# 300 in place of 165 gather slots ahead of the first dense search, 18 in place of 22 among the searches

## The chip, the cores and the metric

The kernel runs on one core of one Trainium2 chip. The metric is the device time of one execution in microseconds (us). The core has TensorE (PE, matmuls and transposes), VectorE (DVE), ScalarE (ACT), GpSimd (POOL), SyncE (SP, which issues most of the DMAs) and 16 DMA engines that all queues share.

## The reference

One decoder layer in float32 for 1,024 tokens of width 1,024: differential attention of 8 heads beside a multi-scale pooling branch, sigmoid gates, an output projection and a first layer norm (the mixer); then PEER, a mixture of 16,384 experts of one neuron each; then a second layer norm. PEER, cut to what matters here:

```python
q = (yb @ w_q).reshape(PEER_CHUNK, PEER_HEADS, 2, PEER_HALF)
s = jnp.einsum('chpk,hpnk->chpn', q, sub_keys).astype(jnp.float32)
s1, i1 = lax.top_k(s[:, :, 0], PEER_TOPK)
s2, i2 = lax.top_k(s[:, :, 1], PEER_TOPK)
cand = (s1[..., :, None] + s2[..., None, :]).reshape(PEER_CHUNK, PEER_HEADS, PEER_TOPK * PEER_TOPK)
sc, ci = lax.top_k(cand, PEER_TOPK)
...
idx = row * PEER_KEYS + col
gate = jax.nn.softmax(sc, axis=-1)
act = jax.nn.gelu(jnp.einsum('ched,cd->che', u[idx], yb), approximate=False)
return jnp.einsum('che,ched->cd', (gate * act).astype(yb.dtype), v[idx])
```

Each token picks 8 x 16 = 128 experts; `u` and `v` have 16,384 rows of 1,024 numbers.

## The kernel before, in words

**Two ways through PEER.** The 1,024 tokens are 8 tiles of 128. The first five tiles (`GT`) take the *gather path*: for one tile, slot 0 to 127 each fetch, for every token of the tile, one expert's `u` and `v` row from HBM into one of the 8 buffers of `ring` (128 rows of 8 KB, about 1 MB), in all 5 x 128 = 640 slots. The last three tiles (`DT`) take the *dense path*: all 16,384 experts are run through TensorE in 128 blocks, and gates that are zero nearly everywhere pick out what counts.

**What a slot costs.** POOL issues the gather (L860) once the slot eight before it has been summed. DVE multiplies and sums the `u` half with the tokens (`product`, L1565); ACT turns the dots of two slots into coefficients (Gelu at L1088, scaling at L1092); DVE adds the scaled `v` half of the slot three before to `z_e` (`add_row`, L1519). Between them DVE runs the steps of the search for the next head's top 16 (`found`, `retrieve`, L1330 to L1401), one search for 16 slots, 24 slots ahead of its first gather.

**The mixer and the dense path.** The mixer runs in three groups of 2, 3 and 3 tiles. For each group PE makes the projections (`units`, L1634, weights `w_in` in three buffers), attention (scores L1680, transposes L1699, values L1719), the branch products (L1751, L1756), the output projection (L1774), and the PEER queries and scores (L1808, L1820, weights `wq` in two buffers that SP refills at L621). In attention DVE takes the logits from PSUM (L1219), waits for ACT's exponentials (L937) at L1228 and mixes the two maps at L1237; in the branches it gates and adds (L1258, L1262, L1266). For the dense path DVE then runs 24 dense searches (`dense_found`) and writes one-hot rows and columns (`dense_hots`, L1446, L1448), from which PE makes the gate matrices (L1850); they go to `g_scr` in HBM. In the last phase PE makes, for each of 128 blocks, `dense_scores` (L1861, 16 instructions, weights `ub`, three buffers, loaded at L710) seven blocks ahead, ACT a Gelu (L1058), DVE the product with the gates (`dense_gates`, L1458), and PE `dense_sums` (L1875, 12 instructions, `vb`, four buffers, L719). The gates come back eight blocks at a time in `gq` (L737, 1.5 MB).

**What sets the order.** The program is one static list for each engine. Everything but the gather path has a due time in *ticks* (`step_at`, `branch_at`, `norm_at`, `score_at`, `sum_at` and others), and each engine's list of it is in order of ticks. The gather path is laid out by slots. `KNOTS`, four pairs (slot, tick), says by straight lines between them which tick a slot stands at (`tick_at`); after each slot every engine's list lets in the other work that is due by then (`advance(tick_at(...))`). So `KNOTS` sets how densely slots lie among the rest, and nothing else. Tick 0 is in the scores of the first group; ticks 7 to 145 hold attention of the second group, 145 to 216 its branches and norm, 216 to 312 its queries; 318 to 505 attention of the third group, 505 to 598 its branches and norm, 598 to 686 its queries; the dense searches run from 616 to 880, the one-hots from 711 to 960 or so, and block b of the dense sums stands at 960 + 9b. The last knot puts slot 640 at tick 2092, 20 before the end of the sums. Each engine works strictly in its list's order.

Of the kernel before, what the change touches and what calls it, by code (L numbers as in the profile page):

```python
# [27 lines left out]
NK = 128  # L28
# [26 lines left out]
LAST_SLOT = SLOTS * GT  # L55
# [46 lines left out]
OH_LEN = 3.5  # L102
T_D = TURN_AT[-1] + 6 + int(OH_LEN * P / NOH) + 14
BLOCK = 9
KNOTS = ((0, 0), (165, 616), (187, 880), (LAST_SLOT, T_D + BLOCK * NK - 20))


def tick_at(t):
    if t <= 0:
        return t  # L110
    for (s0, k0), (s1, k1) in zip(KNOTS, KNOTS[1:]):
        if t <= s1:
            return k0 + (k1 - k0) * (t - s0) / (s1 - s0)
    return KNOTS[-1][1] + t - LAST_SLOT

# [1816 lines left out]
```

How the kernel before makes its waits and increments, by code:

```python
    @block.sync  # L532
# [2 lines left out]
        def units(g):  # L535
            for i in range(UNITS):
                if i < RAWS:
                    yield (T_A[0] - 60 + (2 if i else 0), EARLY + 1, norm_at(1, GTS[1]) + 9)[g]
                    if g == NG - 1 and i == 0:
                        sp.wait_ge(mixed, 2 * KTS[g - 1])
                else:
                    yield unit_at(g, i - RAWS) + 3
                    sp.wait_ge(unit, UNITS * g + i - RAWS + 1)
                kind, j = SEQ[i]
                sp.dma_start(w_raw[g][i % RAWS][:], a["w_in"][FIRST_OF[kind] + j]).then_inc(w_in[g % 2][i % RAWS], 16)
# [1 line left out]
        def tokens(g):  # L547
            yield (T_A[0] - 59, EARLY, norm_at(1, GTS[1]) + 8)[g]
            if g == NG - 1:
                sp.wait_ge(mixed, 2 * KTS[g - 1])
            for c in range(DC):
                sp.dma_start(x_raw[g][:, c],
                             a["xT"][c * P:(c + 1) * P, OLD[g]:OLD[g] + WS[g]]).then_inc(x_all_in if g else x_in[c // 2], 16)
            if g == 0:
                yield unit_at(0, 0)
            elif g == 1:
                yield branch_at(0, DC) + 2
                sp.wait_ge(merge_done, DC)
            else:
                yield norm_at(1, GTS[1]) + 15
                sp.wait_ge(y1_out, 16 * len(PARKED))
# [1 line left out]
            if g == 0:  # L563
                yield unit_at(0, 2)
                sp.wait_ge(bias_made, 2)
                sp.dma_start(b_scr, bias[0][:]).then_inc(bias_in, 16)
# [215 lines left out]
        store(GT - 1)  # L782
        advance(END)
        sp.wait_ge(stored, 16 * TT)
```

## Time and profile before

| | us |
|---|---|
| median of 3 runs | 3548.49 |
| lowest and highest | 3542.34, 3552.24 |
| the profiled execution | 3545.78 |
| its span, first to last instruction | 3544.0 |

Over the span PE is busy 83%, DVE 74%, ACT 26%, POOL 25%, and the DMA engines move 292 GB/s on average. These shares are averages over stages with different limits, so the table of stages has to be read as well as the page. A stage's borders are given in us; the border for a tick is where DVE starts the product of the slot that stands at that tick. Durations of single instructions overlap by some tens of ns where they follow each other at once, so sums over a stretch are taken from the table of stages, which counts overlapping time once.

### The profile page before, as it was taken

To read this page: it belongs to the slowest core of one execution; us is meant where nothing else is said; L and a number is where in the kernel's file an instruction comes from. 1 tells how busy PE (TensorE), PEld (TensorE's weight loads), DVE (VectorE), ACT (ScalarE), POOL (GpSimd) and SP (SyncE) were. 2 spreads that over 40 slices of the span, in tenths; PEclk is the share of its full clock that TensorE was granted. 3 is DMA by queue.
4 is the path that set the end of the run, shared out by engine and by line. 5 is a ranking of instruction groups with operands and counts; after the bars stand their busy time and mean duration, and the time that the engine had idled before them with its cause. 6 is when DMAs were issued, how large, how long until landed. Compare 5 with 4: busy or idle time off the path is not lost.

```text
span 3544.0 us, 32139 instructions
## 1 busy us (share of the span) xinstructions
PE 2943.5 (83%) x9793; PEld 1744.0 (49%) x9793; DVE 2632.1 (74%) x6244; ACT 907.2 (26%) x2305; POOL 882.0 (25%) x866
## 2 busy tenths in 40 slices
PE   9999999979988889785434498878898998889896
PEld 7776665535554554454333354434444444444442
DVE  2224556674666668789999789977889888788888
ACT  2302455122344431223223221211121111112111
POOL 1101223221122322200002223323333233332332
PEclk9999999989999999895655599989999999999998
DMA  6635666787655569633336899999999999999996
GB/s 201 226 122 215 233 225 215 285 325 270 237 195 193 188 246 345 235 125 109 118 127 231 306 417 415 414 381 379 411 410 415 394 402 402 385 394 417 400 415 258
DMA packets 216235, 1034.86 MB, mean 292 GB/s; under 512 B 22400, under 2 KB 60800, under 8 KB 132224
## 3 DMA queue, kind: packets, MB, share of 16 engines
q0 software_dynamic: 92160, 671.13, 48.3%
q1 hardware_dynamic: 122896, 361.54, 27.6%
q8 instruction: 79, 1.29, 0.1%
q14 instruction: 92, 0.75, 0.1%
q10 hardware_dynamic: 1008, 0.14, 0.0%
HBM read 989.21 MB, written 43.52 MB: 291 GB/s over the span
## 4 chain that ended last, share of the span: by engine, by line
PE 58%; DMA 17%; DVE 16%; ACT 3%; SPq 2%; issue 2%; POOL 0%; DVEq 0%; ACTq 0%
PE w_ps L1634 16%; DMA ub<-uT 13%; PE w_ps L1861 13%; PE r_o L1875 7%; PE w_ps L1808 4%; PE w_ps L1875 3%; DVE z_e L1519 3%; DVE hot_r L1446 3%; PE w_ps L1774 2%; DVE hot_c L1448 2%; PE w_ps L1751 2%; DVE ring L1565 2%; DMA ring<-uv,idx 2%; SPq L719 2%; PE r_o L1719 2%
## 5 line engine op out<-in xcount | busy, mean ns | idle before, releaser
L860 POOL DMA_INDIRECT ring<-uv,idx x640 | 739.5, 1155 | 2342.0 <-DVE z_e L1519 2275.3
L1519 DVE SCALAR_TENSOR_TENSOR z_e<-ring,coef,z_e 128x1024 f32<-128x1024 f32 x640 | 820.9, 1283 | 170.0 <-ACT coef L1092 169.5
L1861 PE MATMUL w_ps<-yT,ub 128*128 128x384 f32 x2048 | 715.0, 505 | 163.6 <-DMA ub<-uT 163.6
L1565 DVE CUSTOM_DVE_ANT_0 ring<-ring,ytok 128x1024 f32<-128x1024 f32 x640 | 781.7, 1221 | 66.5 <-DMA ring<-uv,idx 65.5
L1634 PE MATMUL w_ps<-x,w 128*128 128x384 f32 (+1 forms) x2112 | 664.4, 463 | 41.9 <-ACT v L908 22.8
L1861 PEld LDWEIGHTS w_ps<-yT,ub 128*128 128x128 f32 x2048 | 403.9, 198 | 481.2 <-DMA ub<-uT 175.2
L1634 PEld LDWEIGHTS w_ps<-x,w 128*128 128x128 f32 x2112 | 396.3, 194 | 253.2 <-issue 84.6
L1875 PE MATMUL r_o<-vb,gel_d 128*128 128x512 f32 x1024 | 467.0, 599 | 46.0 <-DMA vb<-v 29.6
L1875 PEld LDWEIGHTS r_o<-vb,gel_d 128*128 128x128 f32 x1024 | 196.4, 192 | 270.4 <-issue 209.3
L1850 PE MATMUL r_o<-hot_r,hot_c 128*128 128x128 f32 x768 | 168.9, 409 | 180.1 <-DVE hot_c L1448 180.1
L1058 ACT ACTIVATE gel_d<-w_ps 128x384 f32<-128x384 f32 x128 | 62.6, 489 | 915.3 <-PE w_ps L1861 915.3
L1850 PEld LDWEIGHTS r_o<-hot_r,hot_c 128*128 128x128 f32 x768 | 156.0, 310 | 194.0 <-DVE hot_c L1448 193.8
L1875 PE MATMUL w_ps<-vb,gel_d 128*128 128x512 f32 x512 | 240.6, 592 | 0.0
L1088 ACT ACTIVATE gel<-dot 128x2 f32<-128x2 f32 x320 | 64.0, 200 | 638.9 <-DVE dot L1565 638.3
L1808 PE MATMUL w_ps<-yT,wq 128*128 128x384 f32 x512 | 184.8, 506 | 20.6 <-DMA wq<-wq 10.5
L1875 PEld LDWEIGHTS w_ps<-vb,gel_d 128*128 128x128 f32 x512 | 97.3, 190 | 122.6 <-issue 122.6
L1092 ACT ACTIVATE coef<-gel,gate 128x1 f32<-128x1 f32 x640 | 153.8, 287 | 10.4
L1808 PEld LDWEIGHTS w_ps<-yT,wq 128*128 128x128 f32 x512 | 97.1, 197 | 91.2 <-issue 22.0
L1047 ACT ACTIVATE stage_g<-r_o 128x512 f32<-128x512 f32 x96 | 97.5, 1054 | 167.9 <-PE r_o L1850 167.9
L1446 DVE TENSOR_SCALAR hot_r<-count_d,turned_d 128x128 f32<-128x128 f32 x384 | 135.8, 354 | 0.1
L1219 DVE CUSTOM_DVE_ANT_0 e<-w_ps,bias 128x512 f32<-128x512 f32 (+3 forms) x160 | 90.8, 594 | 60.6 <-PE w_ps L1680 59.0
L1228 DVE RECIPROCAL st_a<-st_a 128x2 f32<-128x2 f32 x64 | 10.5, 164 | 165.0 <-ACT e L937 164.8
(238 smaller groups left out, 2965.1 us busy)
## 6 DMA issues: line engine op xcount, KB each, us to landing
w<-w_in SPq DMA_DIRECT2D x132, 512.0 KB, 3.9
ub<-uT SPq DMA_DIRECT2D x128, 512.0 KB, 11.4
vb<-v SPq DMA_DIRECT2D x128, 512.0 KB, 14.7
g_scr<-stage_g SPq DMA_DIRECT2D x12, 2048.0 KB, 7.7
gq<-g_scr SPq DMA_DIRECT2D x16, 1536.0 KB, 39.7
wq<-wq SPq DMA_DIRECT2D x46, 512.0 KB, 4.7
wc<-w_branch SPq DMA_DIRECT2D x24, 768.0 KB, 5.6
wo<-w_out SPq DMA_DIRECT2D x24, 512.0 KB, 7.8
```

Of the source, the lines that this page charges most:

```text
L860: nc.gpsimd.indirect_dma_start(out=ring[t % RING][:], out_offset=None, in_=a["uv"], in_offset=bass.IndirectOffsetOnAxis(ap=idx[:, slot:slo ...
L1047: nc.scalar.activation(stage_g[c % 2][:, :, 4 * b:4 * b + 4].rearrange("p r t -> p t r"), place_bank(v)[:].rearrange("p (t r) -> p t r", t ...
L1092: nc.scalar.activation(coef[:, slot + j:slot + j + 1], gel[:, slot + j:slot + j + 1], ACT.Copy, scale=gate[:, h, e_:e_ + 1]).then_inc(coef ...
L1219: nc.vector.tensor_tensor_reduce(both[:, wh, c * HALF:c * HALF + n], score_bank(g, wh)[:, 0:n], bias[g][:, begin:begin + n], SCALE, NEG, A ...
L1446: nc.vector.tensor_scalar(hot_r[u % 2][:, j], count_d[:], turned_d[:, 0, t:t + 1], turned_d[:, 2, t:t + 1], ALU.is_equal, ALU.mult)
L1519: nc.vector.scalar_tensor_tensor(z[n % 2][:], ring[t % RING][:, D:], coef[:, slot:slot + 1], z[n % 2][:], ALU.mult, ALU.add).then_inc(vsum ...
L1565: nc.vector.tensor_tensor_reduce(ring[r][:, 0:D], ring[r][:, 0:D], y_of(n)[:], 1.0, 0.0, ALU.mult, ALU.add, dot[:, slot:slot + 1]).then_in ...
L1634: ins = nc.tensor.matmul(bank, w_raw[g][i % RAWS][:, c, :], x_raw[g][:, c, :], start=c == 0, stop=c == DC - 1)
L1808: ins = nc.tensor.matmul(query_bank(g)[:, 0:WS[g]], query_weights(g, i)[:, c * P:(c + 1) * P], yT[g][c // 4][:, c % 4, :], start=c == 0, s ...
L1850: ins = nc.tensor.matmul(place_bank(v)[:, j * NK:(j + 1) * NK], hot_c[u % 2][:, 4 * part + j], hot_r[u % 2][:, 4 * part + j], start=True, ...
L1861: ins = nc.tensor.matmul(dense_bank(b)[:, 0:DENSE], ub[b % NUB][:, c], yT[2][c // 4][:, c % 4, :], start=c == 0, stop=c == DC - 1)
L1875: ins = nc.tensor.matmul(sum_bank(i, half)[:], gel_d[b % NGEL][:, i * P:(i + 1) * P], vb[b % NVB][:, half * HALF:(half + 1) * HALF], start ...
```

## The change

One line, a table of numbers. Its four pairs are (slot, tick):

```diff
 BLOCK = 9
-KNOTS = ((0, 0), (165, 616), (187, 880), (LAST_SLOT, T_D + BLOCK * NK - 20))
+KNOTS = ((0, 0), (300, 616), (318, 880), (LAST_SLOT, T_D + BLOCK * NK - 20))
```

A slot now stands every 2.05 ticks instead of every 3.73 in ticks 0 to 616, every 14.67 instead of 12 in ticks 616 to 880, and every 3.76 instead of 2.68 after tick 880. PE's list is the same row for row. On DVE, ACT, POOL and SP the same work stands in another order; ACT has 164 table loads in place of 154. No instruction of the gather path itself is added or taken away.

**DVE in the second group's attention**, from one step's maximum (L1223) to the reciprocal (L1228) that waits for ACT's exponentials. A slot is one L1565 with its second row and one L1519. Before:

```order
L1223 TENSOR_REDUCE st_a<-st_a 128x2
L1565 ISA ring_222,dot<-ring_222,ytok_168 128x1024
L1565 ISA dot 128x1
L1519 SCALAR_TENSOR_TENSOR z_e_286<-ring_219,coef,z_e_286 128x1024
L1387 TENSOR_REDUCE rc<-hot 128x16
L1228 RECIPROCAL st_a<-st_a 128x2
```

After, two steps later in the same attention (`osb` is an output of attention, L1379 to L1387 are search steps):

```order
L1565 ISA ring_225,dot<-ring_225,ytok_168 128x1024
L1565 ISA dot 128x1
L1519 SCALAR_TENSOR_TENSOR z_e_286<-ring_222,coef,z_e_286 128x1024
L1379 TENSOR_TENSOR hot<-abf,i_296 128x256
L1505 TENSOR_SCALAR gate<-gate,esum 128x16
L1249 TENSOR_SCALAR osb_105<-r_o,st_a 128x128
L1565 ISA ring_226,dot<-ring_226,ytok_168 128x1024
L1565 ISA dot 128x1
L1519 SCALAR_TENSOR_TENSOR z_e_286<-ring_223,coef,z_e_286 128x1024
L1383 TENSOR_TENSOR hot<-hot,topf 128x256
L1565 ISA ring_219,dot<-ring_219,ytok_168 128x1024
L1565 ISA dot 128x1
```

Over the 24 steps of this attention one or two slots stand between L1223 and L1228 before, and one to three after.

**DVE in the third group's branches**, where PE's next product waits until the gates of the last have been made (L1258, L1262). Before, from one sum (L1266) to the next:

```order
L1266 TENSOR_TENSOR gates2a<-gates2a,gates2b 128x384
L1258 SCALAR_TENSOR_TENSOR gates2a<-gates2a,w_ps 128x384
L1565 ISA ring_222,dot<-ring_222,ytok_169 128x1024
L1565 ISA dot 128x1
L1519 SCALAR_TENSOR_TENSOR z_e_287<-ring_219,coef,z_e_287 128x1024
L1360 MAX_INDEX besti<-best,cand 128x8
L1361 MATCH_REPLACE cand_233<-best,cand 128x256
L1364 MAX best<-cand_233 128x8
L1262 SCALAR_TENSOR_TENSOR gates2b<-gates2b,w_ps 128x384
L1266 TENSOR_TENSOR gates2a<-gates2a,gates2b 128x384
```

After, the first part of the same piece:

```order
L1266 TENSOR_TENSOR gates2a<-gates2a,gates2b 128x384
L1565 ISA ring_222,dot<-ring_222,ytok_169 128x1024
L1565 ISA dot 128x1
L1519 SCALAR_TENSOR_TENSOR z_e_287<-ring_219,coef,z_e_287 128x1024
L1360 MAX_INDEX besti<-best,cand 128x8
L1361 MATCH_REPLACE cand_233<-best,cand 128x256
L1364 MAX best<-cand_233 128x8
L1258 SCALAR_TENSOR_TENSOR gates2a<-gates2a,w_ps 128x384
L1565 ISA ring_223,dot<-ring_223,ytok_169 128x1024
L1565 ISA dot 128x1
L1519 SCALAR_TENSOR_TENSOR z_e_287<-ring_220,coef,z_e_287 128x1024
```

Where one slot stood between a sum and the next, three stand now: these two, and a third after L1262.

**DVE in the dense sums**, from one block's product with its gates (L1458) back to the slots before it. Before:

```order
L1565 ISA ring_221,dot<-ring_221,ytok_169 128x1024
L1565 ISA dot 128x1
L1519 SCALAR_TENSOR_TENSOR z_e_287<-ring_226,coef,z_e_287 128x1024
L1383 TENSOR_TENSOR hot<-hot,topf 128x256
L1565 ISA ring_222,dot<-ring_222,ytok_169 128x1024
L1565 ISA dot 128x1
L1519 SCALAR_TENSOR_TENSOR z_e_287<-ring_219,coef,z_e_287 128x1024
L1387 TENSOR_REDUCE rc<-hot 128x16
L1458 TENSOR_TENSOR gel_d_272<-gel_d_272,gq_276 128x384
L1565 ISA ring_223,dot<-ring_223,ytok_169 128x1024
L1565 ISA dot 128x1
```

After, the whole piece from the block before:

```order
L1458 TENSOR_TENSOR gel_d_271<-gel_d_271,gq_276 128x384
L1565 ISA ring_221,dot<-ring_221,ytok_169 128x1024
L1565 ISA dot 128x1
L1519 SCALAR_TENSOR_TENSOR z_e_287<-ring_226,coef,z_e_287 128x1024
L1383 TENSOR_TENSOR hot<-hot,topf 128x256
L1565 ISA ring_222,dot<-ring_222,ytok_169 128x1024
L1565 ISA dot 128x1
L1519 SCALAR_TENSOR_TENSOR z_e_287<-ring_219,coef,z_e_287 128x1024
L1387 TENSOR_REDUCE rc<-hot 128x16
L1458 TENSOR_TENSOR gel_d_272<-gel_d_272,gq_276 128x384
```

Two slots stand between two blocks at this place, where there were three.

## Rows read from the trace of the kernel before

**Rows 1.** The page: span, busy time, 40 slices (clock, DMA share).

```profile
span 3544.0 us, 32139 instructions
...
PE 2943.5 (83%) x9793; PEld 1744.0 (49%) x9793; DVE 2632.1 (74%) x6244; ACT 907.2 (26%) x2305; POOL 882.0 (25%) x866
...
PEclk9999999989999999895655599989999999999998
DMA  6635666787655569633336899999999999999996
```

**Rows 2.** Busy time by stage; columns: stretch, length, busy time (instructions), clock, DMA.

```profile
core 0: us, PE busy (x) PEld busy (x) DVE busy (x) ACT busy (x) POOL busy (x), PEclk, DMA share, GB/s
308.00:492.00 184.00, 183.85 (x774) 121.37 (x773) 100.14 (x259) 78.09 (x192) 38.36 (x49) 1.00 0.67 240
492.00:634.00 142.00, 138.50 (x559) 83.21 (x558) 89.65 (x222) 74.42 (x178) 45.22 (x59) 1.00 0.62 220
634.00:763.00 129.00, 109.79 (x316) 58.51 (x314) 83.86 (x165) 19.95 (x49) 25.90 (x25) 0.94 0.78 290
763.00:900.00 137.00, 124.20 (x418) 75.09 (x419) 82.88 (x158) 29.21 (x78) 30.53 (x26) 0.95 0.82 306
905.00:1045.00 140.00, 118.72 (x461) 68.74 (x461) 82.40 (x197) 59.86 (x126) 29.64 (x35) 0.94 0.60 213
1045.00:1170.00 125.00, 107.38 (x449) 63.30 (x449) 83.64 (x201) 63.28 (x132) 33.03 (x41) 0.95 0.57 195
1170.00:1305.00 135.00, 117.55 (x479) 69.77 (x477) 86.20 (x196) 65.51 (x140) 38.91 (x44) 0.96 0.55 193
1305.00:1369.00 64.00, 60.60 (x183) 35.33 (x184) 50.03 (x102) 5.60 (x20) 17.49 (x18) 0.97 0.98 376
1369.00:1450.00 81.00, 63.20 (x173) 31.39 (x172) 67.02 (x122) 17.23 (x46) 26.93 (x22) 0.87 0.85 321
1450.00:1866.00 416.00, 237.16 (x938) 176.84 (x936) 380.28 (x1488) 105.27 (x181) 21.26 (x22) 0.72 0.36 127
1866.00:2024.00 158.00, 60.52 (x261) 55.11 (x262) 139.92 (x415) 48.63 (x85) 42.29 (x29) 0.54 0.73 263
2024.00:3507.00 1483.00, 1311.39 (x3448) 669.29 (x3446) 1267.71 (x2384) 266.69 (x857) 490.10 (x421) 0.94 1.00 403
```

**Rows 3.** The gate product L1458 and the slots' L1519 in the dense sums, alone.

```profile
2024.00:3507.00 1483.00, 69.66 (x126) 0.94 1.00 403
...
2024.00:3507.00 1483.00, 540.54 (x422) 0.94 1.00 403
```

**Rows 4.** The chain of waits inside the dense sums: start us, us, what.

```profile
2104.40 5.16 PE w_ps L1861 x16
2109.56 3.43 PE r_o L1875 x8
2112.99 1.72 PE w_ps L1875 x4
2114.71 5.16 PE w_ps L1861 x16
...
2214.47 8.25 SPq L719
...
2222.77 34.05 DMA ub<-uT
```

**Rows 5.** DMA in the dense sums: packets, MB, share; issues, KB each, us to landing.

```profile
q0 software_dynamic: 60480, 440.43, 72.4%
q1 hardware_dynamic: 61378, 156.92, 27.5%
...
vb<-v SPq DMA_DIRECT2D x124, 512.0 KB, 16.4
ub<-uT SPq DMA_DIRECT2D x118, 512.0 KB, 12.6
gq<-g_scr SPq DMA_DIRECT2D x14, 1536.0 KB, 39.8
ring<-uv,idx POOLq DMA_INDIRECT x418, 11.8
```

**Rows 6.** DMA issues in the second group's queries (763 to 900 us), us to landing.

```profile
wq<-wq SPq DMA_DIRECT2D x14, 512.0 KB, 6.2
```

**Rows 7.** Waits in the second group's attention and branches (308 to 763 us).

```profile
POOL ring L860 <- DVE z_e L1519: 321.0, 44, 18.4
...
DVE st_a L1228 <- ACT e L937: 75.3, 20, 9.1
ACT aT L950 <- PE w_ps L1699: 40.1, 19, 4.7
DVE osb L1249 <- PE r_o L1719: 29.3, 17, 7.2
DVE e L1219 <- PE w_ps L1680: 27.2, 11, 14.0
```

**Rows 8.** Table loads of ACT at the Gelu of slots, from the page's groups.

```profile
L1088 ACT ACT_TABLE_LOAD x76 | 97.5, 1283 | 1.3
```

## The prediction

> **What bounds the kernel now.** I read the page first. The DMA line of the 40 slices is at 9 from slice 24 to 39, and the clock line dips around slices 19 to 23 [rows 1]: stages with different limits. So the table of stages comes next [rows 2]. From 308 to 900 us PE is the fullest engine (183.85 of 184, 138.50 of 142, 109.79 of 129, 124.20 of 137), and it stays so until 1369 us, where DVE has a third of its time free in attention: 82.40 of 140, 83.64 of 125, 86.20 of 135. From 1450 to 2024 us (dense searches and one-hots) DVE is the limit, 380.28 of 416 and 139.92 of 158, with the DMA engines at 0.36 and 0.73. In the dense sums, 1483 us long, the DMA share is 1.00, PE is busy 1311.39 and DVE 1267.71. That stage is bound by DMA, with PE close behind. The chain there shows how it looks from PE: blocks follow each other every 10.31 us (2104.40 to 2114.71: 5.16 of scores, 3.43 + 1.72 of sums), until a wait for `ub` of 34.05 us after SP has hung 8.25 us in issuing a `vb` load [rows 4]. The transfer in front of them is `gq`, 39.8 us to land, once in eight blocks [rows 5].
>
> **Prices of a slot.** DVE: in the dense sums 1267.71 us less 69.66 of gate products, over 422 slots [rows 2, 3], is 2.84 us a slot, its share of a search included. DMA: the gather queue took 72.4% of 1483 us for 422 slots [rows 3, 5], 2.54 us of all 16 engines a slot. The other queue took 27.5%, 408 us.
>
> **What moves.** Slots per tick change from 0.268 to 0.487 up to tick 616, so the nine stages before 1450 us, of 72, 73, 71, 96, 62, 60, 65, 51 and 60 ticks, get 15.8, 16.0, 15.6, 21.0, 13.6, 13.2, 14.2, 11.2 and 13.2 slots more, 134; one more falls in the 6 ticks between 900 and 905 us, together 300 - 165 = 135. Ticks 616 to 880 lose 4, ticks 880 to 960 lose 29.9 - 21.3 = 8.6, and the dense sums lose the rest, 422 to about 301.
>
> **The dense sums.** DMA needs 408 + 301 x 2.54 = 1173 us. DVE needs 1268 - 121 x 2.84 = 924 us. PE needs 121 blocks of scores at 5.16 and 128 of sums at 3.43 + 1.72, 624 + 659 = 1283 us at the pace of undisturbed blocks [rows 4]. So PE takes over as the limit, and only 200 of the 310 us that DMA gives up can be had. Some of the stall behind `gq` will stay. It costs (1483 - 1311)/14 = 12 us each time now, with the gather queue never empty; with DMA asked for 73 us in the 82 that PE takes for eight blocks, I take 2 us for each of 16, an estimate near the low end, since between the 19 gathers of eight blocks the engines now have gaps that `gq` can use. The ends are 0 and 5 us. That gives 1315 us, a gain of 168 (ends 200 and 120).
>
> **Searches and one-hots.** DVE is the limit, so what it loses comes off: 4 x 2.84 = 11 us and 8.6 x 2.84 = 24 us. What covers nothing here is PE, at 237 of 416 us and 61 of 158 [rows 2]. Gain 35, ends 20 and 37.
>
> **The stages before 1450 us, without attention.** Each gets the time of its fullest resource. Busy DVE time plus 2.84 for each slot more, and DMA share times length plus 2.54 for each:
> 634 to 763 (129 us): DVE 83.9 + 44.3 = 128, DMA 100.6 + 39.6 = 140, so +11.
> 763 to 900 (137 us): DVE 82.9 + 59.6 = 142, DMA 112.3 + 53.3 = 166, so +29.
> 1305 to 1369 (64 us): DVE 50.0 + 31.8 = 82, DMA 62.7 + 28.4 = 91, so +27.
> 1369 to 1450 (81 us): DVE 67.0 + 37.5 = 104, DMA 68.9 + 33.5 = 102, so +23.
> Together +90. The first and third of these hold branches, where three slots now stand between the gates for which PE's products wait: what is queued behind a slot there is PE itself.
>
> **Attention.** Here DVE would need, out of 184, 142, 140, 125 and 135 us, 100.1 + 44.9 = 145, 89.7 + 45.4 = 135, 82.4 + 38.6 = 121, 83.6 + 37.5 = 121 and 86.2 + 40.3 = 127. It fits by the sum, but only if DVE hardly waits, and it works in order: it waits for ACT's exponentials at L1228 (75.3 us in 20 waits), for values at L1249 (29.3) and scores at L1219 (27.2) [rows 7], and PE in turn waits for what stands behind slots on DVE. What share such a mutual chain can reach no row of these stages shows; today it is 0.54 to 0.67. The nearest row in which PE and DVE are both pressed is that of the dense sums, DVE 1268 of 1483, 0.855 [rows 2]. At 0.85 the stages take 171, 159, 142, 142 and 149: 0 + 17 + 2 + 17 + 14 = +50, and since in the first of them PE has no slack at all (183.85 of 184) I add 5% of it, 9. That is +59. The lower end is +10 (DVE fills its time), the upper is below. ACT gets more Gelus between its exponentials, and each change of table is a load of 1283 ns [rows 8]; ten more loads are 13 us, and ACT has at least 62 of 125 us free. The Trainium skill, page "ScalarE: Activation LUTs", section "What ACT_TABLE_LOAD costs", puts a whole switch at about 2.66 us with the drain; by it the ten are 27 us, still beside other work. The trace has a row for the load and none for the drain.
>
> **The sum.** Gains 168 + 35 = 203, losses 90 + 59 = 149: 54 us off. The profiled execution took 3545.8 us, so 3492; the median of the runs lies 2.7 us higher, so I predict 3495.
>
> **Weights that land later.** With the gather queue as full as in the dense sums, a 512 KB load lands after 12.6 to 16.4 us, where `wq` takes 6.2 [rows 5, 6]. With two buffers, two query products need one landing and one product of about 5.16 us: at 12.6 that is 8.9 us each and 142 us for 16, inside the 166 above; at 16.4 it is 173, 7 us more. So it is in the range, not in the sum. The Trainium skill, page "DMA: Bandwidth & Descriptors", section "Queues, rings and completion order", says that each DMA engine goes round the queues that have work, a packet at a time. By that rule the SP queue's loads are slowed wherever gathers are dense, which speaks against the change before 1450 us and for it in the dense sums; it would put the sum at the 173 as well.
>
> **Rivals.**
> *Almost free in front* (0.12). DVE's free third in attention takes the slots, +10 in place of +59, and `gq` leaves no stall (1283): 200 + 35 - 90 - 10 = 135 off, 3413. For it: DVE's work fits by the sum in all five stages. Against it: DVE would have to be 0.95 busy in a chain where it stands at 0.63 now.
> *Lockstep in attention, slower* (0.28). POOL's gather of slot t waits for the sum of t - 8, DVE's sum for ACT's coefficient of three slots ago, and ACT stands in order behind PE. In ticks, these leads shrink by 3.73/2.05: three slots were 11.2 ticks and are 6.2, a little over one step of attention. If DVE reaches only 0.72, the five stages take 201, 188, 168, 168 and 176, +175 in place of +59: 265 - 203 = 62 slower, 3611. The point from which it decides: at 0.77 the stages cost about 115 and gains and losses cancel. For it: today's shares, and waits at L1228 up to 9.1 us [rows 7]. Against it: those waits are long because PE sets the pace, and slots in between fill them.
> *The dense sums do not shrink* (0.06). If the stall behind `gq` comes from `gq` itself and SP's hang and not from gathers, 12 us stay 16 times: 1283 + 192 = 1475, a gain of 8 in place of 168, and the whole is 106 slower, 3655. That would be the change doing nothing where it is meant to. Against it: 39.8 us for 1.5 MB is 40 GB/s, far from the 403 of the stage [rows 2, 5].
>
> **How the numbers follow.** The forecast has 0.54. Its own range is 3430 to 3550: the dense ends (-32, +48), attention from +10 to about the point of balance. Of that, 0.10 lies within 0.3% of before (about what a measurement of this kernel can tell from no change, 11 us) and 0.44 is faster. With the first rival, faster is 0.56; same 0.10; slower 0.28 + 0.06 = 0.34. The range for 8 in 10 must reach the lockstep case: 3430 to 3630. It leaves out most of the first rival and all of the last.
>
> **What would show it.** In the changed profile: dense sums of 1290 to 1340 us with a DMA share below 0.95, a gather count near 301, `gq` landing in under 20 us, and hardly a wait for `ub`; the one-hot stage DVE-bound and 24 us shorter; the start of the dense searches at about 1450 + 149 = 1600 us, with DVE near 0.85 busy in attention and PE below 0.9; `wq` landing in 10 us or more. The prediction is wrong if DVE in attention stays below 0.77, if `ub` waits stay at 12 us each, or if PE's granted clock falls well below the 0.94 to 1.00 of these stages, since its work would then no longer fit between DVE's.

## The result, and the profile after

| | before | changed |
|---|---|---|
| median, us | 3549.26 | 3436.98 |
| lowest to highest | 3542.34 to 3552.24 | 3435.76 to 3438.46 |
| span of the profiled execution | 3544.0 | 3435.3 |

The ratio is 0.9687 with a 95% interval of 0.967 to 0.9703: 112 us faster, where 54 were forecast. The direction was right and the time lies in the range; the forecast gain was half of what came.

The page of the changed kernel, against [rows 1]:

```profile
span 3435.3 us, 32149 instructions
...
PE 2934.8 (85%) x9793; PEld 1738.0 (51%) x9793; DVE 2622.9 (76%) x6244; ACT 915.9 (27%) x2315; POOL 907.7 (26%) x866
...
PEclk9999999997998989988966655999999999999999
DMA  6635888899987777998322257999999999999995
```

The work is the same to a fraction of a per cent; where it lies has changed. DMA is now at 7 to 9 from slice 5 to 19, and the last block of high DMA share is shorter. The table of stages of the changed kernel, with borders at the same ticks as in [rows 2], shows how much each stage has grown or shrunk:

```profile
core 0: us, PE busy (x) PEld busy (x) DVE busy (x) ACT busy (x) POOL busy (x), PEclk, DMA share, GB/s
308.00:496.00 188.00, 185.23 (x777) 121.81 (x776) 143.93 (x344) 93.77 (x226) 56.56 (x64) 1.00 0.88 321
496.00:653.00 157.00, 144.52 (x570) 86.15 (x568) 134.94 (x310) 91.25 (x216) 71.31 (x76) 0.99 0.83 302
653.00:796.00 143.00, 111.60 (x308) 58.32 (x309) 127.91 (x251) 25.03 (x73) 41.94 (x41) 0.90 0.97 386
796.00:955.00 159.00, 131.31 (x422) 78.22 (x421) 141.57 (x266) 39.00 (x113) 55.91 (x48) 0.91 1.00 401
966.00:1123.00 157.00, 119.17 (x444) 67.20 (x443) 126.28 (x284) 66.91 (x153) 49.69 (x50) 0.88 0.79 282
1123.00:1257.00 134.00, 105.71 (x438) 62.51 (x439) 119.57 (x263) 72.23 (x159) 56.97 (x56) 0.91 0.81 288
1257.00:1398.00 141.00, 119.79 (x473) 70.42 (x471) 119.90 (x265) 66.65 (x156) 56.91 (x57) 0.92 0.77 274
1398.00:1490.00 92.00, 68.55 (x189) 38.07 (x189) 85.99 (x176) 12.50 (x42) 27.61 (x28) 0.89 0.99 405
1490.00:1595.00 105.00, 72.65 (x182) 35.89 (x183) 103.17 (x193) 25.90 (x72) 40.76 (x35) 0.81 0.96 376
1595.00:1995.00 400.00, 227.60 (x921) 170.10 (x920) 366.74 (x1460) 98.51 (x165) 17.62 (x19) 0.74 0.33 124
1995.00:2133.00 138.00, 58.32 (x260) 53.68 (x260) 118.11 (x369) 46.18 (x73) 27.16 (x20) 0.55 0.67 240
2133.00:3398.00 1265.00, 1265.00 (x3424) 651.57 (x3425) 910.70 (x1707) 201.29 (x642) 363.30 (x298) 1.00 0.95 369
```

| stage | before | after | forecast growth | measured |
|---|---|---|---|---|
| five attention stages | 726 | 777 | +59 | +51 |
| branches, norm, queries of group 2 (129, 137) | 266 | 302 | +40 | +36 |
| branches, norm and first queries of group 3 (64, 81) | 145 | 197 | +50 | +52 |
| the 6 ticks between (5) | 5 | 11 | 0 | +6 |
| dense searches and one-hots | 574 | 538 | -35 | -36 |
| dense sums | 1483 | 1265 | -168 | -218 |

The sum is -109, the difference of the spans. The last row is nearly all of the miss. There PE is now busy 1265.00 of 1265 us at a granted clock of 1.00, and DMA is down to 0.95. Its DMA rows and waits, against [rows 5]:

```profile
q0 software_dynamic: 42768, 311.45, 62.7%
q1 hardware_dynamic: 59775, 154.24, 32.6%
...
vb<-v SPq DMA_DIRECT2D x123, 512.0 KB, 8.2
ub<-uT SPq DMA_DIRECT2D x118, 512.0 KB, 7.5
gq<-g_scr SPq DMA_DIRECT2D x14, 1536.0 KB, 16.2
ring<-uv,idx POOLq DMA_INDIRECT x296, 9.3
```

```profile
DVE z_e L1519 <- ACT coef L1092: 349.6, 94, 7.0
...
PE r_o L1875 <- DMA vb<-v: 28.6, 1, 28.6
```

The gate load lands in 16.2 us instead of 39.8, `ub` in 7.5 instead of 12.6, and the wait of PE for `ub` (34.05 us on the chain in [rows 4]) has left the list; one wait for the first `vb` is left, which ends where the stage begins. DVE's 349.6 us of idle time before L1519 are the room that it now has.

For the forecast it matters how many blocks of sums (L1875, 12 instructions a block) lie inside the stage. Before, and after:

```profile
2024.00:3507.00 1483.00, 672.93 (x1512) 288.08 (x1510) 0.94 1.00 403
...
2133.00:3398.00 1265.00, 660.36 (x1488) 283.68 (x1489) 1.00 0.95 369
```

That is 126 blocks before and 124 after, of 128.

### The profile page after: what moved, and what is told of

Its sections match the earlier page's. It is cut to its first block, busy times and chain, and to the rows that moved or that the text cites. A ratio compares the mean times of both kernels' runs of the same rounds, so it can differ in the third digit from the quotient of the medians.

```text
span 3435.3 us, 32149 instructions
## 1 busy us (share of the span) xinstructions
PE 2934.8 (85%) x9793; PEld 1738.0 (51%) x9793; DVE 2622.9 (76%) x6244; ACT 915.9 (27%) x2315; POOL 907.7 (26%) x866
## 3 DMA queue, kind: packets, MB, share of 16 engines
q1 hardware_dynamic: 122896, 361.54, 28.3%
## 4 chain that ended last, share of the span: by engine, by line
PE 65%; DVE 23%; DMA 6%; ACT 3%; issue 3%; SPq 0%; POOL 0%; DVEq 0%; ACTq 0%; POOLq 0%
PE w_ps L1861 19%; PE w_ps L1634 14%; PE r_o L1875 13%; PE w_ps L1875 6%; DVE z_e L1519 5%; DVE ring L1565 4%; PE w_ps L1808 3%; DVE hot_r L1446 3%; DVE hot_c L1448 2%; PE r_o L1808 2%; DMA ring<-uv,idx 2%; PE r_o L1719 1%; DMA wq<-wq 1%; PE w_ps L1680 1%; PE w_ps L1774 1%
## 5 line engine op out<-in xcount | busy, mean ns | idle before, releaser
L860 POOL DMA_INDIRECT ring<-uv,idx x640 | 752.1, 1175 | 2234.4 <-DVE z_e L1519 2173.6
L1519 DVE SCALAR_TENSOR_TENSOR z_e<-ring,coef,z_e 128x1024 f32<-128x1024 f32 x640 | 819.0, 1280 | 359.4 <-ACT coef L1092 359.2
L1565 DVE CUSTOM_DVE_ANT_0 ring<-ring,ytok 128x1024 f32<-128x1024 f32 x640 | 779.6, 1218 | 13.7 <-DMA ring<-uv,idx 13.7
L1634 PE MATMUL w_ps<-x,w 128*128 128x384 f32 (+1 forms) x2112 | 672.4, 467 | 61.0 <-ACT v L908 34.5
L1861 PE MATMUL w_ps<-yT,ub 128*128 128x384 f32 x2048 | 683.6, 488 | 0.0
L1861 PEld LDWEIGHTS w_ps<-yT,ub 128*128 128x128 f32 x2048 | 390.3, 191 | 297.4 <-issue 60.3
L1875 PE MATMUL r_o<-vb,gel_d 128*128 128x512 f32 x1024 | 462.6, 595 | 28.6 <-DMA vb<-v 28.6
L1875 PEld LDWEIGHTS r_o<-vb,gel_d 128*128 128x128 f32 x1024 | 195.3, 191 | 248.9 <-issue 187.9
L1875 PE MATMUL w_ps<-vb,gel_d 128*128 128x512 f32 x512 | 240.6, 592 | 0.0
L1875 PEld LDWEIGHTS w_ps<-vb,gel_d 128*128 128x128 f32 x512 | 97.3, 190 | 122.4 <-issue 122.4
L1751 PE MATMUL w_ps<-o,wc 128*128 128x384 f32 x256 | 93.3, 520 | 19.3 <-DMA wc<-w_branch 9.6
```

Of the source, the lines that this page charges most:

```text
L860: nc.gpsimd.indirect_dma_start(out=ring[t % RING][:], out_offset=None, in_=a["uv"], in_offset=bass.IndirectOffsetOnAxis(ap=idx[:, slot:slo ...
L1519: nc.vector.scalar_tensor_tensor(z[n % 2][:], ring[t % RING][:, D:], coef[:, slot:slot + 1], z[n % 2][:], ALU.mult, ALU.add).then_inc(vsum ...
L1565: nc.vector.tensor_tensor_reduce(ring[r][:, 0:D], ring[r][:, 0:D], y_of(n)[:], 1.0, 0.0, ALU.mult, ALU.add, dot[:, slot:slot + 1]).then_in ...
L1634: ins = nc.tensor.matmul(bank, w_raw[g][i % RAWS][:, c, :], x_raw[g][:, c, :], start=c == 0, stop=c == DC - 1)
L1751: ins = nc.tensor.matmul(bank, branch_weights(g, n)[:, j, :], o_all[g][:, j, :], start=j == 0, stop=j == CA - 1)
L1861: ins = nc.tensor.matmul(dense_bank(b)[:, 0:DENSE], ub[b % NUB][:, c], yT[2][c // 4][:, c % 4, :], start=c == 0, stop=c == DC - 1)
```

## The experiments

The reasons to be tested: (A) each stage is as long as its fullest resource; the dense sums cost the larger of PE's floor and the DMA demand of 408 us + 2.54 us a slot. (B) the stalls behind `gq` are a cost of their own. For attention: DVE's load, or the lockstep of the engines, or ACT's table switches. Each run makes one edit to the changed kernel or to the one before; one run joins two of them.

### One part of the change at a time

```diff
-KNOTS = ((0, 0), (300, 616), (318, 880), (LAST_SLOT, T_D + BLOCK * NK - 20))
+KNOTS = ((0, 0), (300, 616), (322, 880), (LAST_SLOT, T_D + BLOCK * NK - 20))
```

> One part of the change alone: 300 slots ahead as in the change, but 22 among the dense searches as before. Searches are bound by DVE, so 4 slots more cost 4 x 2.84 = 11 us there; the dense sums lose 4 slots and are bound by PE, so they stay at 1265. Theory A: 3448 us. A rival in which slots among the searches fill idle time of DVE: 3437, no difference.

Measured 3447.62 us (3442.54 to 3451.51), ratio 0.9721 (0.9696 to 0.9745). The stage of the searches is 409 us long against 400, with 22 slots against 18; the dense sums 1267 us. That is theory A. The intervals of the two kernels overlap a little, so the row of the stage carries this more than the time does.

```diff
-KNOTS = ((0, 0), (300, 616), (318, 880), (LAST_SLOT, T_D + BLOCK * NK - 20))
+KNOTS = ((0, 0), (165, 616), (183, 880), (LAST_SLOT, T_D + BLOCK * NK - 20))
```

> The other part alone: 165 slots ahead as before, 18 among the searches as in the change. The search stage loses 11 us, the dense sums, bound by DMA there, get 4 slots of 2.54 us, 10 us. Theory A: 3548 us, no difference from before. The rival that the middle number is worth 11 us by itself: 3538.

Measured 3548.07 us over 10 runs, ratio 1.0005 (0.9993 to 1.0017). The searches (ticks 616 to 880) take 403 us instead of 416, the 422 slots of the dense sums become 425 in 1489 us and the one-hots 162 instead of 158. So the same four slots are worth about 10 us when the dense sums are bound by PE and nothing when they are bound by DMA: the small second number of the change only pays because of the first.

### How many slots in front

```diff
-KNOTS = ((0, 0), (300, 616), (318, 880), (LAST_SLOT, T_D + BLOCK * NK - 20))
+KNOTS = ((0, 0), (262, 616), (280, 880), (LAST_SLOT, T_D + BLOCK * NK - 20))
```

> The changed kernel with 262 slots ahead of tick 616 instead of 300, 18 among the searches as in the change. Theory A (the dense sums cost the larger of PE's floor, 1265 us as in the changed kernel, and the DMA demand of 408 us plus 2.54 us a slot): about 336 slots are left there, 408 + 853 = 1261 us, so the stage stays at 1265 to 1280. The stages ahead get 38 slots fewer, and by each stage's fullest resource they cost about 67 to 80 us more than in the kernel before instead of 145. Together 3360 to 3380 us, faster than the changed kernel. Rival B (the stall behind the gate loads comes back as soon as the gather queue is nearly always busy, and a slot in front costs a flat 1.07 us): dense sums 1300 us or more, front cheaper by 41, together 3425 to 3440.

> The changed kernel with 230 slots ahead of tick 616. Theory A: about 366 slots are left in the dense sums, 408 + 930 = 1338 us, DMA-bound; the stages ahead cost about 30 us more than in the kernel before instead of 145. Together 3437 - 115 + 73 = 3395 us (3380 to 3410). Rival B: dense sums of 1350 us, front cheaper by 75 only, together 3447.

> Between front262 and the change: 275 slots ahead, evenly. Dense sums of about 324 slots: 408 + 823 = 1231 of DMA against 1265 of PE, so 1265 to 1278 us; stages ahead between 80 (at 262) and 145 us (at 300) above before, about 102. Together 3400 to 3410 us: no gain over front262, which puts the best even density between 250 and 275.

| slots in front | time, us | ratio to before (95%) | growth in front | dense sums (slots) |
|---|---|---|---|---|
| 165 (before) | 3548.38 | 1 | 0 | 1483 (422) |
| 230 | 3448.32 | 0.9717 (0.9694 to 0.9740) | +63 | 1338 (365) |
| 262 | 3395.01 | 0.9563 (0.9538 to 0.9587) | +80 | 1285 (335) |
| 275 | 3396.98 | 0.9568 (0.9548 to 0.9588) | +99 | 1272 (323) |
| 300 | 3436.98 | 0.9687 (0.9670 to 0.9703) | +145 | 1265 (299) |

front275 came out as expected (3400 to 3410 us, 1265 to 1278 in the dense sums, +102 in front) but for 3 us, and can't be told from front262. front262 was expected at 3360 to 3380 us and came 15 above.

In the dense sums theory A holds at 230 slots: 408 + 366 x 2.54 = 1338 was expected and 1338 came, with 365 slots. Near the crossing, where PE and DMA both ask for about 1260, the stage is about 25 us above either:

```profile
2075.00:3360.00 1285.00, 1273.78 (x3436) 654.49 (x3437) 1010.27 (x1897) 218.94 (x704) 409.74 (x334) 1.00 0.99 393
```

That row is front262, and this is front230, where DMA is the limit again:

```profile
2071.00:3409.00 1338.00, 1283.19 (x3440) 657.96 (x3440) 1101.03 (x2064) 234.66 (x758) 427.98 (x364) 0.98 1.00 402
```

In front theory A misses: at 230 it expected +30 and +63 came. That is 33 of the 53 us by which the kernel was slower than expected; 15 more are one-hots (ticks 880 to 960, 153 us with 25 slots against 138 with 21), which the expectation had left out, and 5 are searches (405 against 400). Of the +63, attention has 39 (765 against 726), the branch, norm and query stages 24. At 300 slots attention has 51, these stages 88. So the two kinds grow differently: the stages near their DMA or DVE limit slowly at first and then steeply (+24, +42, +88 for 65, 97 and 135 more slots in all), attention with three quarters of its growth in the first half of the slots (+39, +36, +51). A stage of attention still grows where slots are laid denser than that, as the last experiment shows.

### Are the stalls behind the gate loads a cost of their own?

In the kernel before, from the third on, the gate loads are left out:

```diff
-                sp.dma_start(gq[q % 2][:].rearrange("p c r t -> p c (r t)"),
-                             g_scr[:, :, GQ * q:GQ * (q + 1), :].rearrange("c p r t -> p c (r t)")).then_inc(g_in[q % 2], 16)
+                if q < 2:
+                    sp.dma_start(gq[q % 2][:].rearrange("p c r t -> p c (r t)"),
+                                 g_scr[:, :, GQ * q:GQ * (q + 1), :].rearrange("c p r t -> p c (r t)")).then_inc(g_in[q % 2], 16)
...
-                    dve.wait_ge(g_in[b // GQ % 2], 16 * (b // GQ // 2 + 1))
+                    dve.wait_ge(g_in[b // GQ % 2], 16)
```

> The kernel before with the 14 later gate loads (gq, 1.5 MB each) left out of the dense sums; the gates of the first 16 blocks are used again and again, so that part of the output isn't the reference's. Theory A (the stage is bound by the DMA engines' total): the gate loads are 22 of the 157 MB of their queue, about 57 of its 408 us, so the dense sums fall from 1483 to about 1425 us and the time to about 3490. Rival B (the stalls behind gq are a cost of their own, 172 us of idle PE): PE's floor shows, 1265 to 1310 us in the dense sums, time 3330 to 3380.

Measured 3464.65 us (3460.51 to 3468.79) beside 3552.29, ratio 0.9753 (0.9697 to 0.9809). The stage, between the same two slots as in [rows 2]:

```profile
2031.00:3430.00 1399.00, 1312.42 (x3447) 659.53 (x3446) 1273.56 (x2384) 265.02 (x857) 443.82 (x421) 0.98 1.01 412
```

It is 84 us shorter and still has a DMA share of 1.01, with 87 us of idle PE although no gate load is left. So theory B falls as it was priced: its 1265 to 1310 us did not come. What it said of the place of the stalls was right, though. These are the page's rows of the whole kernel (its lines stand one lower in the file: L1862 is L1861 elsewhere, L1876 is L1875):

```profile
L1566 DVE CUSTOM_DVE_ANT_0 ring<-ring,ytok 128x1024 f32<-128x1024 f32 x640 | 780.4, 1219 | 125.0 <-DMA ring<-uv,idx 123.4
...
L1862 PE MATMUL w_ps<-yT,ub 128*128 128x384 f32 x2048 | 684.1, 488 | 0.0
L1876 PE MATMUL r_o<-vb,gel_d 128*128 128x512 f32 x1024 | 495.3, 629 | 123.4 <-DVE gel_d L1459 93.5
```

PE waits for `ub` no more (163.6 us in 14 waits in the dense sums before), and `ub` and `vb` land in 8.0 and 7.9 us instead of 12.6 and 16.4. In their place PE waits for DVE's product with the gates, 86.1 us in 47 waits of the stage, while DVE is busy 1273.56 of its 1399 us and waits 119.6 for gathers. So the loads behind `gq` were where the shortage showed first; with `gq` gone it shows at the gathers, and half of PE's idle time stays. In the kernels with `gq` PE's wait for `ub` grows with the shortage: none at 299 slots, 8.1 us at 335, 54.8 at 365 and 163.6 at 422.

Theory A's price for the load was too low. It took 1.5 MB as bytes (4.1 us). The time of the queue's packets fell from 27.5% of 1483 us to 24.3% of 1399, by 68 us or 4.9 a load; the stage fell by 84 us, 6.0 a load. What the other 16 us are stays open. The packets are smaller than others: the queue's count, over the whole kernel, fell from 122896 to

```profile
q1 hardware_dynamic: 101168, 339.52, 26.4%
```

that is by 21728 packets for 22 MB, 1 KB each, while the gathers' 440.43 MB in 60480 packets [rows 5] are 7.3 KB each on average. In the trace of the kernel before a packet of 1 KB takes 48 ns of its engine in this stage and one of 8 KB from a gather 318 ns, so the same bytes take 1.2 times as long in the small ones, and the 1,536 packets of a load 4.6 us of 16 engines.

### What bounds the dense sums once PE is lighter?

```diff
-                for i in range(DT):
+                for i in range(DT if b in (0, NK - 1) else DT - 1):
```

> The changed kernel with PE's sums of the third dense tile left out in 126 of 128 blocks (1.72 of 10.31 us of PE work a block), which leaves that tile's output wrong. Theory A: PE's floor in the dense sums falls to about 1055 us, below the DMA demand of 408 + 299 x 2.54 = 1167 us, so the stage goes from 1265 to about 1170 to 1190 us, with a DMA share of 1.00, and the time to about 3350. Rival B (stalls of the weight loads return as soon as PE waits for nothing else): 1230 us or more. If PE had not been the limit at all: 1265, no difference.

Measured 3374.15 us (3368.45 to 3379.84), ratio 0.9499 (0.9425 to 0.9572).

```profile
2135.00:3329.00 1194.00, 1086.78 (x2948) 569.96 (x2947) 908.64 (x1706) 202.52 (x642) 355.41 (x298) 0.95 0.98 391
```

The stage is 1194 us long, 4 above the upper end of theory A and 27 above the demand of 1167, with the DMA share at 0.98; the whole is 24 us above the 3350 expected. PE is busy 1086.78 us of it and waits the other 107.2 for `ub`. So PE was the limit in the changed kernel, and DMA is next, 70 us below. Here `gq` takes 29.0 us to land where the changed kernel needs 16.2.

### What lengthens attention?

```diff
-                nc.vector.tensor_tensor_reduce(ring[r][:, 0:D], ring[r][:, 0:D], y_of(n)[:], 1.0, 0.0, ALU.mult,
+                nc.vector.tensor_tensor_reduce(ring[r][:, 0:HALF], ring[r][:, 0:HALF], y_of(n)[:, 0:HALF], 1.0, 0.0, ALU.mult,
```

> The changed kernel with the product of each slot made over 512 of 1024 columns (L1565), which halves an operation of about 1.15 us and leaves half of each dot out. It takes about 0.57 us from DVE for each slot and nothing from DMA. Theory A (each stage ahead is as long as its fullest resource): attention, bound by DVE at a busy share of about 0.9, gives back what it lost, 188, 157, 157, 134, 141 to about 184, 143, 143, 127, 136; the stages with a DMA share of 0.97 to 1.00 (143, 159, 92 us) stay; 105 falls to about 95; searches and one-hots lose 22. Together about 3437 - 85 = 3352 us. Rival C (the lockstep of engines, not DVE's load, makes attention longer): attention stays within 10 us in sum, time about 3405. The dense sums stay at 1265 in both.

```diff
-            nc.scalar.activation(gel[:, slot:slot + GROUP], dot[:, slot:slot + GROUP], ACT.Gelu).then_inc(gelu_out, 1)
+            nc.scalar.activation(gel[:, slot:slot + GROUP], dot[:, slot:slot + GROUP], ACT.Copy).then_inc(gelu_out, 1)
```

> The changed kernel with the Gelu of the slots' dots (L1088) made a plain copy, which leaves the Gelu of the first five tiles out; ACT then has 44 table loads (1283 ns each) in place of 164, and DVE, PE and DMA have the same work. Theory T (attention lengthens because the switches of table stand in front of the exponentials that DVE waits for): the attention stages return from 188, 157, 157, 134, 141 to about 184, 143, 142, 126, 136, the whole to about 3390. Theory D (what counts is DVE's load and the slots in front of PE's inputs on DVE): attention keeps all but 10 us of its length, the whole 3425 to 3437. The dense sums stay at 1265 in both.

Both edits in one kernel:

> The changed kernel with both cuts at once: the product of a slot over half its columns, and a copy for the Gelu of the slots (both leave part of the first five tiles' result out). The five attention stages, 777 us together in the changed kernel and 726 in the kernel before, were 748 with the first cut and 755 with the second. If DVE's load and ACT's table switches are delays that add up in one chain, they come to 726 (720 to 732). If both only shorten the same wait, so that one hides the other, they stay at 740 or more. The whole: about 3437 - 56 - 19 = 3362 in the first case, 3375 or more in the second.

| kernel | time, us | ratio (95%) | five attention stages | sum |
|---|---|---|---|---|
| before | 3549.26 | 1 | 184, 142, 140, 125, 135 | 726 |
| changed | 3436.98 | 0.9687 (0.9670 to 0.9703) | 188, 157, 157, 134, 141 | 777 |
| half product | 3380.80 | 0.9517 (0.9476 to 0.9558) | 187, 149, 149, 128, 134 | 747 |
| no Gelu | 3417.78 | 0.9630 (0.9602 to 0.9658) | 185, 152, 153, 127, 138 | 755 |
| both | 3358.63 | 0.9440 (0.9399 to 0.9480) | 184, 146, 138, 123, 134 | 725 |

Each of the two theories, DVE's load alone and table switches alone, expected nearly the whole of the 51 us from its own cut, and got 30 and 22; the times, 3380.80 and 3417.78, lie between the two expectations in both runs. Together they give back 52: in sum nothing of the growth is left, though the kernel still has 300 slots in front and as many gathers on the DMA engines as the changed one (a share of 0.87 in the first stage). So in attention it isn't the gathers' traffic by itself. What the runs cut was a slot's work on DVE (0.54 of its 2.84 us) and, every other slot, a Gelu's table loads on ACT. The reading that fits is that this work stands as a delay in front of the work for which PE waits. This is the second of the attention stages in the kernel with half products, in the columns of [rows 2]; in the changed kernel it is the row from 496 to 653 us above:

```profile
494.00:643.00 149.00, 143.34 (x573) 85.79 (x571) 116.33 (x310) 90.98 (x218) 63.74 (x76) 1.00 0.86 316
```

DVE has 33 us free in it and ACT 58, and the stage is still 7 us longer than the 142 of before. A limit by one engine's load doesn't explain that; delays in a chain would. This last step is argued: both cuts take away load and delay together, and no run moved the same slots to other places between the waits. How much falls on which wait stays open too.

### Is the growth local to its stage?

```diff
-KNOTS = ((0, 0), (300, 616), (318, 880), (LAST_SLOT, T_D + BLOCK * NK - 20))
+KNOTS = ((0, 0), (35, 72), (55, 145), (90, 216), (140, 318), (190, 505), (244, 616), (262, 880), (LAST_SLOT, T_D + BLOCK * NK - 20))
```

> The changed kernel with the slots of the attention stages (ticks 72 to 145 and 318 to 505) at the density of before (20 and 50 instead of 36 and 91) and all others as dense as in the change, 244 ahead of tick 616. Local theory (a stage's length follows from what lies in it): the four attention stages return from 157, 157, 134, 141 to 142, 140, 125, 135 us, the others stay at 188, 143, 159, 92, 105; about 353 slots in the dense sums take 1305 us, together about 3440. Spill theory (the engines enter attention late or out of step because of the dense stages around it): attention stays longer than before by over half of what it lost, 3460 or more.

Measured 3427.38 us (3421.60 to 3428.63), ratio 0.9650 (0.9628 to 0.9672). The four stages with the old density take 145, 138, 123 and 138 us, 544 together against 542 before and 589 in the changed kernel; the dense ones around them stay at 189, 144, 164, 84 and 103. The growth is local, and the spill theory falls. The whole is 13 us under the 3440 expected, 7 of them in the dense sums (352 slots in 1298 us). The first of the four, with busy times close to those of [rows 2]:

```profile
496.00:641.00 145.00, 138.55 (x561) 83.40 (x560) 91.11 (x224) 74.60 (x178) 45.48 (x59) 1.00 0.63 220
```

### A layout by what each stage has free

```diff
-KNOTS = ((0, 0), (300, 616), (318, 880), (LAST_SLOT, T_D + BLOCK * NK - 20))
+KNOTS = ((0, 0), (43, 72), (76, 145), (106, 216), (142, 312), (144, 318), (174, 380), (200, 440), (230, 505),
+         (244, 556), (265, 616), (283, 880), (LAST_SLOT, T_D + BLOCK * NK - 20))
```

> 265 slots ahead, laid by what each stage has free: 43, 33, 30, 36, 2, 30, 26, 30, 14, 21 in place of the even density of front262 (30, 31, 30, 41, 3, 26, 26, 27, 22, 26), then 18 among the searches. Theory A as first held (fullest resource, DVE at 0.9 in attention): the stages ahead cost 20 to 40 us more than in the kernel before, 3345 us. Theory A2 (attention lengthens by its first few slots more and then stays, as in front230, front262 and the change, 153 to 157 us and 155 to 158 us): only the branch, norm and query stages gain, about 10 us against front262, 3385 us.

Measured 3383.44 us (3379.79 to 3389.78), ratio 0.9527 (0.9507 to 0.9548), 168 us below the kernel before and 54 below the changed one. It is the fastest complete kernel of the study. Against front262 its interval overlaps, so a gain over an even layout is likely and not shown.

The time is theory A2's and its mechanism is not. The branch, norm and query stages gained 20 us against front262 (132, 152, 66 and 83 against 136, 145, 82 and 90), twice the 10 expected. Attention did not stay: its five stages take 196, 157, 159, 139 and 135 us, 786 together against 762 in front262 and 777 in the changed kernel, with 162 slots in them against 140 and 161. The first stage alone paid for its 43 slots with 196 us. So the nine stages in front take 2 us more than in front262, and nothing was won there; the dense sums, 332 slots in 1271 us against 335 in 1285, gave the difference. That the sum met 3385 is luck.

## Why the prediction was right and wrong, step by step

**What bounds the kernel, and the prices.** Right. DMA bound the dense sums: in before_no_gq the time fell with the DMA work while PE and DVE still had idle time, and the stage shrank with the gathers from 422 to 365 slots. 2.84 us a slot on DVE gave 924 us for the dense sums and 910.70 were measured; 2.54 us a slot of DMA gave 1338 us at 230 slots and 1338 came. The second queue's 408 us was taken from a row and needed no price for `gq`. The sum of the two is a floor, not the time: at 335 slots and with the lighter PE the stage came out about 25 us above it.

**The stages in front.** +149 forecast, +145 measured, and each group within 8 us. For branches, norm and queries the rule of the fullest resource was sound, and the rows of the changed kernel show the DMA shares of 0.96 to 1.00 that it asked for. For attention the number was near (+59 against +51) and the reason was not shown to be right: no fixed cap on DVE's share fits the runs. DVE reached 0.86, 0.80, 0.89 and 0.85 in the four stages after the first, around the 0.85 taken, but at 230 slots it stood at 0.75 (115.88 of 154) in a stage that had grown nearly as much. That 0.85, lent by the row of the dense sums, came so near in the changed kernel is in part luck; by the same rule front230 was costed 33 us too low in front.

**Searches and one-hots.** -35 forecast, -36 measured (-16 and -20, where -11 and -24 were forecast).

**The dense sums.** This is the step that failed: 1315 us forecast, 1265 measured. That DMA would give way to PE was right; the sizes of two terms were wrong. First, PE's floor was sized at 128 blocks of sums and set against a stage that does not hold them. The stage of 1483 us ends where DVE starts the last slot: 126 blocks of sums lie in it before, and only 124 after, because the last four stand behind DVE's last slot, in the 37 us to the end of the span that both kernels have. 121 x 5.16 + 124 x 5.15 = 1263 us is the floor of that stretch, 20 less than 1283. All 128 blocks, from the first sum to the last, took PE 1505 us before (2023.0 to 3527.7) and 1286 after (2133.0 to 3419.0): the 1283 was a right floor for them, and it had to be taken from 1505. Second, 32 us of stalls behind `gq` were added (2 us for each of 16), and they came as nothing: PE was busy 1265.00 of 1265 us, with no wait for `ub`. 20 + 32 is the miss of 50, less the 2 us by which 1265 lies above 1263. The low end (a gain of 200) allowed for the second and not for the first.

**The share of `gq`'s stall.** "It costs 12 us each time now" read the waits as the price of one transfer. before_no_gq shows less: 6.0 us of the stage for each load left out. The rest was the shortage of DMA, which shows at the loads behind `gq` as long as they are there.

**Rivals.** Lockstep at 0.72 did not come, but delays between engines that wait in turn, its mechanism, are the reading that the cuts in attention leave, at a lower price. "The dense sums do not shrink" is refuted, by the result and by before_no_gq. "Almost free in front", with a chance of 0.12, was wrong in attention (+51 where it had +10) and right that `gq` would leave no stall; its 3413 us lies 24 below the 3437 measured, the forecast's 3495 lies 58 above. The sentence on weights that land later is settled too: `wq` in the second group's queries landed in 8.5 us instead of 6.2, below the 12.6 that would have left the sum as it was, and the stage took 159 us against 166. The Trainium skill's rule of engines that go round the queues (page "DMA: Bandwidth & Descriptors", section "Queues, rings and completion order") fits both signs seen here, `wq` later where gathers are dense and `gq` 39.8 to 24.0 to 16.2 us where they thin out; the traces show the times, not the rule, and the 173 us that the prediction drew from it for the queries did not come. The table loads were costed at nothing, 13 us beside other work. Taking 120 of them away brought 19 us of the whole: a load that has cover by busy time still cost time, and it did so in attention, where DVE waits for ACT's exponentials: those five stages fell by 22 us.

**Signs named ahead.** The start of the dense searches (1595 us, about 1600 named), 299 slots, `gq` in 16.2 us and the missing waits for `ub` came. The dense sums (1290 to 1340 named) and `wq` (10 us or more named, 8.5 measured) did not, nor did the 24 us of the one-hots quite (20).

## What to carry to other kernels

Work that can be laid anywhere belongs where the resource that it uses is free, and only as much of it as makes the crowded stage hit its next limit: here that was near 335 slots in the dense sums. The 36 slots moved beyond that took 20 us off the dense sums (1285 to 1265) and put 65 on the stages in front (+80 to +145), and the whole was 42 us slower. Find that point from two rows, the fullest resource and the next, before moving, and count the next one's work inside exactly the stretch that you compare; a stretch that ends with one engine's work holds another share of a second engine's work once that engine falls behind. In stages where engines wait for each other in turn, busy shares give a floor only; pieces put between the links can lengthen the stage even when every engine has time to spare.

## What the hardware showed that was not expected

- A load of 1.5 MB in 1 KB packets took 4.6 to 4.9 us of packet time on all 16 DMA engines, and the stage shrank by 6.0 us for each one left out, beside gathers in which 1.05 MB took 2.54. By the byte that is 1.2 to 1.3 times the gathers' price in packet time, and 1.6 times in the stage.
- Its landing time moved far more: 39.8 us in the kernel before, 29.0 in after_less_pe, 24.0 in front262, 16.2 in the changed kernel. The DMA share alone does not order these times (1.00, 0.98, 0.99, 0.95; and 21.5 us at 1.00 in shaped265). What does stays open.
- In the third group's first attention stage the granted clock fell from 0.94 to 0.88 when slots were laid denser, with PE busy 119 us in both, of 140 and of 157. The clock is unlikely to be what lengthens it: in attention_as_before the same stage had 0.90 and took 138 us.
